# Two request groups through two trunk layers: slot rows read two blocks ahead, result rows in two buffers, blocks taken in pairs in the expert stage

## The reference

```python
def moe_ffn(h, router_w, router_bias, w_gate, w_up, w_down):
    ...
    _, eidx = lax.top_k(jnp.where(emask, sel, -jnp.inf), TOP_K)      # 2 of 16 experts
    ...
    hg = jnp.einsum('td,edf->tef', t, w_gate)
    hu = jnp.einsum('td,edf->tef', t, w_up)
    act = jax.nn.silu(hg) * hu * comb[:, :, None].astype(t.dtype)
    return jnp.einsum('tef,efd->td', act, w_down).reshape(B, L, D)
...
x = layer_norm(ALPHA * x + g2 * y, P['ln_w'][l, 1], P['ln_b'][l, 1])
```

## Time and profile before

| What | Value |
|---|---|
| Median of 3 runs | 1385.99 us (1384.95 to 1388.35) |
| Profiled execution, its own time | 1387.69 us |
| Its span, first to last instruction | 1386.0 us |
| PE, PEld, DVE, ACT, POOL busy, share of the span | 74%, 41%, 30%, 19%, 8% |
| Expert stage of layer 0, first row read to last down product | 368 to 667 us |
| Expert stage of layer 1, the same | 1038 to 1346 us |
| Moved from and to HBM | 319.70 MB read, 23.23 MB written |

### The profile page before, as it was taken

The page is one execution under the profiler, slowest core; times in us unless marked ns, Lnnn a source line. Parts: engine busy times, 40 slices in busy tenths (PEclk is TensorE's granted clock), DMA queues, the critical chain, the costliest instruction groups (busy, mean ns, idle before and its releaser), DMA issues.

```text
span 1386.0 us, 23542 instructions
## 1 busy us (share of the span) xinstructions
PE 1025.2 (74%) x9358; PEld 573.8 (41%) x9358; DVE 412.2 (30%) x1120; ACT 262.3 (19%) x456; POOL 107.8 (8%) x168
## 2 busy tenths in 40 slices
PE   1899996896368655778569999889748788876540
PEld 0444455645234323444235554435434444443220
DVE  0310128806211111112354234551631222111106
ACT  0401012502122211223122111110222222222111
POOL 1100001100200000000220000000010000000012
PEclk9999998996699878999879999999858999988785
DMA  9975334394396999993995104636421938799983
GB/s 322 372 255 182 129 117 150 120 426 167 121 386 231 390 411 404 401 349 128 348 377 217 61 16 139 240 122 262 163 93 36 369 129 328 275 396 404 411 338 136
DMA packets 78264, 343.83 MB, mean 248 GB/s; under 512 B 7783, under 2 KB 8362, under 8 KB 65917
## 3 DMA queue, kind: packets, MB, share of 16 engines
q1 hardware_dynamic: 57108, 289.16, 54.0%
q0 software_dynamic: 13152, 42.92, 9.0%
q10 hardware_dynamic: 7944, 10.88, 2.4%
HBM read 319.70 MB, written 23.23 MB: 247 GB/s over the span
## 4 chain that ended last, share of the span: by engine, by line
PE 43%; DMA 34%; DVE 11%; issue 6%; ACT 2%; SPq 2%; ACTq 1%; POOL 1%; POOLq 0%; DVEq 0%
DMA slot_rows<-arena 11%; PE bank L575 10%; PE bank L800 9%; PE bank L740 7%; DMA arena<-in_moe_w_up_dram 6%; DMA arena<-slot_rows 5%; DMA ring<-in_moe_w_up_dram 5%; DMA ring<-in_ada_w_dram 4%; PE bank L747 4%; PE bank L698 3%; DMA arena<-in_ln_b_dram 2%; PE bank L528 2%; SPq L1151 1%; PE bank L874 1%; PE bank L897 1%
## 5 line engine op out<-in xcount | busy, mean ns | idle before, releaser
L740 PE MATMUL bank<-ring,arena 128*32 128x256 f32 x3008 | 189.1, 408 | 35.0 <-DMA ring<-in_moe_w_up_dram 32.8
L740 PEld LDWEIGHTS bank<-ring,arena 128*32 128x32 f32 x3008 | 103.1, 119 | 116.8 <-issue 60.3
L575 PE MATMUL bank<-ring,hT 128*128 128x512 f32 x336 | 144.9, 593 | 1.0 <-ACT hT L933 1.0
L800 PE MATMUL bank<-hT,ring 128*128 128x384 f32 x384 | 124.6, 487 | 1.0 <-ACT hT L933 1.0
L747 PE MATMUL bank<-ring,arena 128*32 128x256 f32 x1504 | 105.7, 428 | 23.5 <-DVE arena L1121 23.5
L1119 DVE TENSOR_TENSOR arena<-arena,bank 128x64 f32<-128x64 f32 x134 | 27.0, 201 | 287.8 <-ACT arena L1038 287.8
L733 PE MATMUL bank<-keep,arena 64*128 64x64 f32 x276 | 31.9, 239 | 103.6 <-DMA arena<-slot_rows 103.6
L1038 ACT ACT_TABLE_LOAD x67 | 86.0, 1283 | 105.6 <-issue 97.5
L740 PE MATMUL bank<-arena 128*32 128x256 f32 x1280 | 82.7, 416 | 24.6 <-DMA arena<-in_moe_w_up_dram 24.6
L575 PEld LDWEIGHTS bank<-ring,hT 128*128 128x128 f32 x336 | 63.6, 190 | 80.5 <-issue 79.3
L800 PEld LDWEIGHTS bank<-hT,ring 128*128 128x128 f32 x384 | 72.7, 190 | 52.5 <-ACT hT L933 1.2
(11 more groups left out here) (285 smaller groups left out, 1014.1 us busy)
## 6 DMA issues: line engine op xcount, KB each, us to landing
ring<-in_ada_w_dram SPq DMA_DIRECT2D x24, 2048.0 KB, 15.2
ring<-in_moe_w_gate_dram SPq DMA_DIRECT2D x22, 2048.0 KB, 20.9
ring<-in_moe_w_up_dram SPq DMA_DIRECT2D x22, 2048.0 KB, 23.9
ring<-in_moe_w_down_dram SPq DMA_DIRECT2D x22, 2048.0 KB, 25.4
arena<-in_moe_w_gate_dram SPq DMA_DIRECT2D x10, 2048.0 KB, 24.0
arena<-in_moe_w_up_dram SPq DMA_DIRECT2D x10, 2048.0 KB, 29.3
arena<-in_moe_w_down_dram SPq DMA_DIRECT2D x10, 2048.0 KB, 29.6
ring<-in_ev_w_in_dram SPq DMA_DIRECT2D x7, 2048.0 KB, 15.7
```

The source lines that it names most:

```text
L575: last = pe.matmul(bank[3 * (c % 2) + t], hT[:, k, t * P:(t + 1) * P], slot8(n)[:, k, :], start=k == 0, stop=k == KT - 1)
L740: last = pe.matmul(bank[1][q * BLK:(q + 1) * BLK, 0:HALF], slot_inT[:, k, :], both[:, :, k, q * P:(q + 1) * P], start=k == 0, stop=k == KT ...
L800: last = pe.matmul(bank[c % 3][:, 0:T], slot8(n)[:, k, (c % 4) * P:(c % 4 + 1) * P], hT[:, k, :], start=k == 0, stop=k == KT - 1)
```

## The change

- `slot_rows` is read into two buffers `slot_ahead`, each with its own semaphore (`row_in0`, `row_in1`), for the blocks of even and odd number. POOL waits for a read to land and for TensorE's transposes, does a one-column addition, copies the buffer (64x512) to `slot_in` and then issues the read of the block two further on into the buffer just copied. PE waits for the copy (`row_rdy`), no longer for the transfer.
- `slot_out` becomes two buffers, with a semaphore each (`stored0`, `stored1`). The copies out of the bank wait for the store of two blocks before.
- ACT, DVE and POOL loop over pairs of blocks, with two blocks written out in the body. DVE computes the numbers of pairs (`trips`). Where the number of blocks is odd (layer 0 here), ACT and DVE run one more block without data behind the last, for which PE raises the semaphores, and its store goes to unused rows. Where it is even (layer 1), POOL makes one more pair.
- `slot_rows` has two blocks more, and is zeroed in 11 transfers where there were 7.
- The loops of PE and the issue of the weights stay as they were.

```diff
-        slot_out = at(4224, 512, rows=2 * BLK)
+        slot_out = [at(4224, 512, rows=2 * BLK), at(6400, 512, rows=2 * BLK)]
+        slot_ahead = [at(5376, 512, rows=2 * BLK), at(5888, 512, rows=2 * BLK)]
...
-            row_halves(0)
-            with pool.Fori(1, blocks + 1) as b:
-                pool.wait_ge(S["rowT_mm"], b)
-                row_halves(b)
+            def rows_ahead(block, odd):
+                pool.dma_start(slot_ahead[odd], slots[bass.ds(block * BLK, BLK), :].rearrange("s (h c) -> (s h) c", h=2)).then_inc(S[f"row_in{odd}"], 16)
+
+            rows_ahead(0, 0)
+            rows_ahead(1, 1)
+            with pool.Fori(0, pairs) as pair:
+                for odd in range(2):
+                    pool.wait_ge(S[f"row_in{odd}"], pair * 16 + 16)
+                    pool.wait_ge(S["rowT_mm"], pair * 2 + (odd + 1))
+                    pool.tensor_tensor(idle, wsel[:, 0, 0:1], wsel[:, 0, 0:1], ALU.add)
+                    pool.tensor_copy(slot_in, slot_ahead[odd]).then_inc(S["row_rdy"], 1)
+                    pool.wait_ge(S["row_rdy"], pair * 2 + (odd + 1))
+                    rows_ahead(pair * 2 + (odd + 2), odd)
...
-            pool.wait_ge(S["row_in"], blocks * 16 + 16)
-            pool.wait_ge(S["slot_stored"], blocks * 32 + 32)
+            for odd in range(2):
+                pool.wait_ge(S[f"row_in{odd}"], pairs * 16 + 16)
+            for odd in range(2):
+                pool.wait_ge(S[f"stored{odd}"], stores * 32 + 32)
...
-                wait_counted(pe, S["row_in"], rows_due, 16)
+                wait_counted(pe, S["row_rdy"], rows_due, 1)
...
+            pe.sem_inc(S["rowT_mm"], 1)
             rows_to_channels()
...
-            pe.wait_ge(S["rowT"], blocks + 1)
-            pe.wait_ge(S["evac_dve"], blocks + 1)
-            pe.wait_ge(S["evac_act"], blocks + 1)
+            pe.wait_ge(S["down_mm"], blocks)
+            for name in ("gu_mm", "rowT_mm", "down_mm"):
+                pe.sem_inc(S[name], 1)
+            stores = pe.value_load(trips[0:1, 1:2], min_val=NE // 2, max_val=MAX_BLOCKS // 2)
+            pe.wait_ge(S["rowT"], stores * 2 + 1)
+            pe.wait_ge(S["evac_dve"], stores * 2 + 1)
+            pe.wait_ge(S["evac_act"], stores * 2 + 1)
...
-            with act.Fori(0, blocks) as b:
-                act.wait_ge(S["gu_mm"], b + 1)
+            with act.Fori(0, pairs) as pair:
+                for odd in range(2):
+                    act.wait_ge(S["gu_mm"], pair * 2 + (odd + 1))
...
-                act.wait_ge(S["slot_stored"], b * 32 + 32)
-                act.activation(slot_out[:, HALF:2 * HALF], bank[5][2 * BLK:4 * BLK, 0:HALF], ACT.Copy).then_inc(S["evac_act"], 1)
+                    act.wait_ge(S[f"stored{odd}"], pair * 32 + 32)
+                    act.activation(slot_out[odd][:, HALF:2 * HALF], bank[5][2 * BLK:4 * BLK, 0:HALF], ACT.Copy).then_inc(S["evac_act"], 1)
...
+            pairs_f = rt(12, 2)
+            for k, rest in enumerate((0.75, 0.25)):
+                link(dve.tensor_scalar(pairs_f[:, k:k + 1], base[:, NE:NE + 1], 0.5, rest, ALU.mult, ALU.add))
+            link(dve.tensor_scalar(pairs_f, pairs_f, ROUND, None, ALU.add))
+            link(dve.tensor_scalar(pairs_f, pairs_f, ROUND, None, ALU.subtract))
+            dve.tensor_copy(trips[0:1, :], pairs_f[0:1, :]).then_inc(trips_rdy, 1)
```

More of the change, by code:

```diff
@@ L1046, in act_moe @@
-            act.wait_ge(S["down_mm"], blocks)
+            pairs = act.value_load(trips[0:1, 1:2], min_val=NE // 2, max_val=MAX_BLOCKS // 2)
+            with act.Fori(0, pairs) as pair:
+                for odd in range(2):
+                    act.wait_ge(S["gu_mm"], pair * 2 + (odd + 1))
+                    act.activation(silu_g, bank[1][:, 0:P].rearrange("p (r f) -> p f r", f=FT), ACT.Silu).then_inc(S["silu"], 1)
+                    act.wait_ge(S["down_mm"], pair * 2 + (odd + 1))
+                    act.wait_ge(S[f"stored{odd}"], pair * 32 + 32)
+                    act.activation(slot_out[odd][:, HALF:2 * HALF], bank[5][2 * BLK:4 * BLK, 0:HALF], ACT.Copy).then_inc(S["evac_act"], 1)
+                    act.wait_ge(S["evac_act"], pair * 2 + (odd + 2))
+                    act.wait_ge(S["evac_dve"], pair * 2 + (odd + 2))
+                    for h in range(2):
+                        act.dma_start(slots[bass.ds((pair * 2 + odd) * BLK, BLK), h * 512:(h + 1) * 512],
+                                      slot_out[odd][h * BLK:(h + 1) * BLK, :]).then_inc(S[f"stored{odd}"], 16)
@@ L1119, in gated @@
                 dve.tensor_tensor(act_rows[:, two, :], silu_g[:, two, :], up, ALU.mult).then_inc(S["gated"], 1)
-                dve.wait_ge(S["gated"], b * 2 + (half + 1))
+                dve.wait_ge(S["gated"], pair * 4 + (2 * odd + half + 1))
                 dve.transpose(act_T[:, two, :].rearrange("p f s -> p (f s)"),
@@ L1124, in dve_moe @@
             dve.sem_inc(S["evac_dve"], 1)
-            dve.wait_ge(S["rowT_mm"], 1)
+            dve.wait_ge(S["rowT_mm"], 2)
             rows_in()
-            with dve.Fori(0, blocks) as b:
-                dve.wait_ge(S["silu"], b + 1)
-                gated(b, 0)
-                gated(b, 1)
-                dve.wait_ge(S["rowT_mm"], b + 2)
-                rows_in()
-                dve.wait_ge(S["down_mm"], b + 1)
-                dve.wait_ge(S["slot_stored"], b * 32 + 32)
-                dve.tensor_copy(slot_out[:, 0:HALF], bank[5][0:2 * BLK, 0:HALF]).then_inc(S["evac_dve"], 1)
+            with dve.Fori(0, pairs) as pair:
+                for odd in range(2):
+                    dve.wait_ge(S["silu"], pair * 2 + (odd + 1))
+                    gated(pair, odd, 0)
+                    gated(pair, odd, 1)
+                    dve.wait_ge(S["rowT_mm"], pair * 2 + (odd + 3))
+                    rows_in()
+                    dve.wait_ge(S["down_mm"], pair * 2 + (odd + 1))
+                    dve.wait_ge(S[f"stored{odd}"], pair * 32 + 32)
+                    dve.tensor_copy(slot_out[odd][:, 0:HALF], bank[5][0:2 * BLK, 0:HALF]).then_inc(S["evac_dve"], 1)
         @block.sync
@@ L1215, in gpsimd_program @@
             rows = slots.rearrange("(b r) n -> r b n", r=BLK)
-            for b in range(0, MAX_BLOCKS + 2, ZERO_STEP):
+            for b in range(0, MAX_BLOCKS + 4, ZERO_STEP):
                 pool.dma_start(rows[:, b:b + ZERO_STEP, :],
```

42 lines of the change are left out of this document (20 added, 22 removed).

## The result

The changed kernel takes **1352.0 us** (median of 4 runs, 1346.9 to 1357.5) against 1387.2 for the kernel before in the same session: ratio 0.9745, 95% interval 0.9701 to 0.9790. Two repeats gave 1353.4 (6 runs, ratio 0.9743, 0.9705 to 0.9780) and 1350.7 (5 runs, 0.9714, 0.9680 to 0.9748). The prediction was 1344, range 1328 to 1374.

The account below looks back on a forecast made before the run. Weights set the pace in full DMA windows; in the holes weights wait for blocks, held by slot reads and stores. Gains of 24 us (layer 0) and 18 (layer 1) sum to 42, from 1386.0 to 1344 us, range 1328 to 1374.

Parts of the forecast that it names:

- Two loops of more than 8 us hold the blocks: Expert blocks behind weights: row-read loop and result-store loop each take more than 8 us round, while PE needs 6.32.
- The copy: POOL's new row copy per block: taken as 1.2 us; up to 4.5 us costs nothing, hidden between two PE transposes.
- The start: First block of each layer: PE waits for read, addition and copy, costing 1.5 us once per layer (0.5 to 2.8).
- Layer 0: Expert stage of layer 0: hole at 434 closes, expert 6 released at 430, last expert's first down product 24 us earlier.
- Layer 1: Blocks 6 to 19 of layer 1 take 88.5 us instead of 108.0; all after expert 7's issue 18 us earlier.
- The dummy block: Layer 0's extra block without data: 4 to 5 us before POOL gathers, hidden, costed at nothing (bound 2 us).
- The end: End of layer 1: constant rows issued 15 us later; weights gain 1 to 2, gathers lose likewise: 0 (-2 to +4).
- DVE held by POOL's copy: Rival, block loop: DVE stalls during POOL's copy, 0.7 us on each of 32 blocks, 22 us, giving 1366; chance 0.12.
- Landings that grow with the pace: Rival, reads and stores: at 12 us a landing, blocks run at about 7.5, 35 us lost, 1379; chance 0.08.
- POOL's copy paces the blocks: Rival, block loop: each microsecond of copy above 4.5 goes into about 45 blocks; 1450 at 7 us; chance 0.03.
- The gain hidden anyway: Rival, weight stream: a hole closed in one place might open in another, 1382 to 1390; chance 0.05.
- More than 42: Rival, whole kernel: fewer PE gaps spare the slower clock, odd block has no table load, 1320 to 1330; chance 0.06.

Follow-up runs that it names:

- the two halves of the change: Changed kernel's double-buffered result rows alone, put on the kernel before: 1387.4 us; changed kernel with one result buffer and semaphore, row reads still two ahead: 1405.9, again 1402.5.
- five copies: Changed kernel with four extra copies of the same rows per block on POOL, each with its own wait and one-column addition: 1356.1 us.
- nine copies: Changed kernel with eight extra copies of the same rows per block on POOL, each with its own wait and one-column addition: 1445.4 us, ratio 1.0399.
- the experiment with the constants: Changed kernel with POOL issuing the four LayerNorm constant rows ahead of the odd half of its last pair, not behind: 1346.1 us, again 1344.1.
- half the weights: Changed kernel in which experts 3 to 15 load only half of each matrix, so the output is not the reference's: 1228.2 us.

## Why the prediction was right, step by step

- **Two loops of more than 8 us hold the blocks.** Shown by the two halves of the change: each loop alone still holds the block at 8.2 to 8.4 us in layer 0 (7.7 and 7.9 in layer 1), and only both together give 6.32.
- **The copy.** Taken as 1.2 us between 0.19 and 2.34; the group of L490 has 599/599/626 ns, 70 times. It did not matter: up to 4.0 us stay hidden, as "a copy of up to 4.5 us costs nothing" said. What decides first is not PE's wait but POOL's own round, 1.2 us longer than its computing, because the issue of the read stands in it. It is 5.2 us with five copies (401.87 to 407.99, less 0.94 idle) and 8.5 with nine, so by an estimate from these two it reaches 6.32 at about 5.1 us of computing; no run lies between 4.0 and 7.3.
- **The start.** Predicted 1.5 per layer. From the first read's issue to PE's first products of layer 0 5.52 us pass instead of 4.47 (366.69 to 372.21 against 368.05 to 372.52): 1.05. With the copy at 0.6 my own working would have said 0.9.
- **Layer 0.** Expert 6 was predicted at 430.0 and came at 429.48 (433.79 and 430.37 in the repeats, as their stages began later). The last expert's first down product was predicted at 609.5, decided by weights over PE; it stands at 607.15 and waited for its weights:

```profile
607.15 1.93 PE L762 MATMUL bank<-ring,arena 128*32 128x256 f32 x32 [1.80 <-DMA ring<-in_moe_w_down_dram]
```

  24 us were predicted. The last down product is 26.3 earlier, of which 1.4 lie ahead of the stage, so 25.0. The working had a slip: 447.4 less 436.7 is 10.7 and not 10.5. And the 0.6 us of the stream's time that each block was to cost do not show: the window from 379 to 434 moved 380 GB/s with the denser blocks, 373 before.
- **Layer 1.** 19.5 on the fourteen blocks as predicted. With the start counted (first row read to the issue of expert 7, 131.9 against 150.6 us) it is 18.7, where 18 were predicted. "Expert 7 of layer 1 issued near 1170" left out that layer 0 ends 24 us earlier; with that it is 1146.5, and 1144.33 came.
- **The dummy block.** PE idles 3.6 us between the last down product and its next products, until DVE's dummy copy is done, instead of 1.3, and yet it transposes the LayerNorm's rows (692.02) 53.3 us after the last down product, where it was 53.8 before (718.81). Hidden, as predicted.
- **The end.** Predicted 0 (-2 to +4), measured +3.6 in this profile and 5.6 and 7.9 in the repeats (96.6 and 98.9 us from expert 15 to the end against 91.0). This is the term that was wrong, in size and in both of its parts. "The weights gain 1 to 2 us": they gained nothing. The last gate and up products begin 43.3 us after expert 15's issue before and 43.3 to 43.5 after; then they take 6.3 to 6.5 us instead of 5.2, at a lower granted clock (below), so the last down product comes 1.2 to 1.4 us later. "The gathers queue behind the rows and lose about as much": the gathers lost nothing, the last store did, and with it 2.4 to 6.5 us ahead of the LayerNorm, as the experiment with the constants shows. The version with early constants gives back 4.7 of it, and adds a gain in layer 0 that the kernel before did not have.
- **The sum.** 42 predicted, 41.0 between the profiles, 35 to 39 between the medians. That the profile comes within 1 us of the forecast is in part luck: it lies 5.1 below the median of its four runs, with the earliest stage of the three (378.9, against 383.2 and 379.8) and the shortest end. The medians lie 8.0, 9.4 and 6.7 us above 1344; in the profiles of the two repeats the end alone takes 5.6 and 7.9.

The rivals. *DVE held by POOL's copy*: refuted. With nine copies POOL is at work nearly all the time, and DVE's multiplications and transposes there last as long as in the changed kernel. First the changed kernel, then nine copies, from 378 to 640 us:

```profile
L1151 DVE STREAM_TRANSPOSE arena<-arena 128x64 f32<-128x64 f32 x66 | 16.2, 246 | 2.3
...
L1149 DVE TENSOR_TENSOR arena<-arena,bank 128x64 f32<-128x64 f32 x66 | 13.3, 202 | 166.1 <-ACT arena L1060 166.1
```

```profile
L1155 DVE STREAM_TRANSPOSE arena<-arena 128x64 f32<-128x64 f32 x54 | 13.2, 245 | 1.9
...
L1153 DVE TENSOR_TENSOR arena<-arena,bank 128x64 f32<-128x64 f32 x54 | 10.9, 202 | 129.3 <-ACT arena L1064 129.3
```

246 and 245 ns, 202 and 202; the copy to `slot_out` takes 417 in both. Only the copy of the transposed rows takes 419 ns instead of 386, and there it follows a wait for PE; in the kernel before, where nothing of POOL's computing stands beside it, it took 406. By the Trainium skill, SBUF — State Buffer, "Who interferes with whom", a DVE instruction with at most one SBUF input, outside the two-port modes, does not contend with GpSimd. Here the trace agrees for the multiplications and transposes. *Landings that grow with the pace*: medians 7.0 and 6.7 where they were 6.9 and 6.4. *POOL's copy paces the blocks*: not at 0.60 us. Its price came close: 1450 was worked out for a copy of 7 us (1386 + 1.5 x 45 is 1453.5), and the kernel with 7.3 us took 1445. In part two slips offset each other, since the threshold is nearer 5.1 us of computing than 4.5 and the base 1352 and not 1344; the 93 us above 1352, at 8.47 - 6.32 a block, are 43 blocks where 45 were counted. *The gain hidden anyway*: both closed holes stayed gains. *More than 42*: the granted clock in the full windows is 0.87 and 0.83, hardly other than 0.84 and 0.83, and the profile gives 41. The stated range was said to take in most of the second rival, but its 1379 lies outside 1374.

## What to carry to other kernels

A wait that stands in the list with 180 us can be worth nothing: two loops of like length ran side by side, and taking one away left the time as it was, taking the other away made it 1% longer, and both together made it 2.5% shorter. So write down the round time of every loop that passes through a block, and change all those above the wanted pace at once. An added stage in a pipeline is free up to a threshold; count the issue of its transfer into its round. And look at what a longer loop pushes back behind it, and beside which small transfer that lands: here four loads of constants, whose move ahead of the last block was worth another 7 us.

## What the runs showed of the hardware

- A 64x512 f32 copy on POOL takes 0.60 us; a dependent addition and copy repeat every 0.81. From the copy's end to the issue of the read that waits for it 0.68 us pass in the mean of 70, 1.0 at most, and no larger cost of changing between computing and issuing shows.
- A row read of 128 KB beside the weight stream lands after 7.0 us in the median, 2.3 at best, whether it is issued every 8.5 or every 6.3 us.
- A store of 64 KB beside four loads of 512 KB issued at the same moment landed after 4.1 to 7.9 us, and after 1.6 in the kernel before, where they had gone out 17 us ahead of it.
- 64 gate and up matmuls take 3.64 us at a granted clock of 1.00, 4.94 at 0.73 (first run with the constants early), 5.24 at 0.69 and 6.51 at 0.55. The last two, behind waits of 8.87 and 7.55 us, before and after, with the windows of the same stretches:

```profile
1338.28 5.24 PE L740 MATMUL bank<-ring,arena 128*32 128x256 f32 x64 [8.87 <-DMA ring<-in_moe_w_up_dram]
1338.20:1343.50 5.30, 5.22 (x65) 2.54 (x65) 0.00 (x0) 0.00 (x0) 0.00 (x0) 0.69 0.99 408
...
1293.72 6.51 PE L755 MATMUL bank<-ring,arena 128*32 128x256 f32 x64 [7.55 <-DMA ring<-in_moe_w_up_dram]
1293.70:1300.20 6.50, 6.48 (x65) 3.02 (x65) 0.00 (x0) 0.00 (x0) 0.00 (x0) 0.55 0.34 142
```

- With half the weights, where PE hardly waits, the granted clock is 0.98 and the pace stays 6.32.
- Executions of one kernel spread by 5 to 8 us to either side of their median (1348.2 to 1361.4 about 1353.4 in six runs). One profile against one profile is good to that, whatever the decimals of its rows say.
